# Starting the expert scatter one up-projection slab earlier, in a kernel for two transformer blocks

## The reference, cut to what matters

```
u   = expert_u[experts]                       # (256, 128, 1024)
act = gelu(einsum('td,tkd->tk', x, u)) * gates
out = einsum('tk,tkd->td', act, expert_v[experts])
```

## Time and profile before

| | us |
|---|---|
| median of three runs | 1771.59 |
| lowest, highest | 1768.38, 1773.86 |
| profiled execution, its time | 1774.22 |
| profiled execution, its span | 1772.6 |
| TensorE busy in the span | 1700.1 (96%) |
| VectorE, ScalarE busy | 1304.3 (74%), 1023.6 (58%) |
| first and last scatter matmul start | 525.3, 764.5 |
| mean granted TensorE clock | 0.987 |

### The profile page before, as it was taken

The page is one execution under the profiler, slowest core; times in us unless marked ns, Lnnn a source line. Parts: engine busy times, 40 slices in busy tenths (PEclk is TensorE's granted clock), DMA queues, the critical chain, the costliest instruction groups (busy, mean ns, idle before and its releaser), DMA issues.

```text
span 1772.6 us, 34483 instructions
## 1 busy us (share of the span) xinstructions
PE 1700.1 (96%) x10902; PEld 1530.1 (86%) x10902; DVE 1304.3 (74%) x2376; ACT 1023.6 (58%) x1567; POOL 119.5 (7%) x105
## 2 busy tenths in 40 slices
PE   7999999999999999999999999998999998899997
PEld 6998889999999999988888888897878887778886
DVE  5865755599977777767777777777777676877776
ACT  6753445566656666655445545663476666666665
POOL 0012300143320000000000000000000000000000
PEclk9998999999999999999999999999999999999999
DMA  5442246476775555567787777542345655246553
GB/s 189 163 158 72 82 138 212 150 230 199 218 236 176 177 175 172 172 206 241 244 270 243 239 244 242 172 150 84 107 155 192 196 181 158 84 131 201 190 186 111
DMA packets 114411, 316.65 MB, mean 179 GB/s; under 512 B 12752, under 2 KB 45904, under 8 KB 113840
## 3 DMA queue, kind: packets, MB, share of 16 engines
q1 hardware_dynamic: 113504, 311.88, 54.5%
q0 software_dynamic: 848, 4.00, 0.7%
HBM read 296.95 MB, written 18.87 MB: 178 GB/s over the span
## 4 chain that ended last, share of the span: by engine, by line
PE 82%; DVE 10%; ACT 4%; issue 2%; DMA 1%; POOL 1%; ACTq 0%; DVEq 0%; SPq 0%
PE bank L309 10%; PE bank L310 10%; PE bank L311 10%; PE bank L259 9%; PE bank L260 9%; PE bank L281 9%; PE bank L261 9%; PE bank L285 5%; PE bank L1302 3%; DVE wlo L243 2%; PE bank L1744 1%; ACT whi L235 1%; PE bank L1009 1%; POOL wlo L1601 1%; DVE arena L2023 1%
## 5 line engine op out<-in xcount | busy, mean ns | idle before, releaser
L243 DVE TENSOR_TENSOR wlo<-raw,whi 128x1024 fp32r<-128x1024 f32 x495 | 608.3, 1230 | 160.5 <-ACT whi L235 150.3
L235 ACT ACTIVATE whi<-raw 128x1024 fp32r<-128x1024 f32 x524 | 550.1, 1051 | 33.0 <-PE bank L303 20.5
L259 PE MATMUL bank<-x,whi 128*128 128x256 f32 (+1 forms) x1728 | 510.3, 295 | 8.9 <-DVE wlo L243 4.0
L261 PE MATMUL bank<-x,wlo 128*128 128x256 f32 (+1 forms) x1728 | 493.8, 286 | 0.0
L260 PE MATMUL bank<-x,whi 128*128 128x256 f32 (+1 forms) x1728 | 493.5, 286 | 0.0
L259 PEld LDWEIGHTS bank<-x,whi 128*128 128x128 f32 x1728 | 333.8, 193 | 15.2 <-issue 13.1
L260 PEld LDWEIGHTS bank<-x,whi 128*128 128x128 f32 x1728 | 334.2, 193 | 0.1
L261 PEld LDWEIGHTS bank<-x,wlo 128*128 128x128 f32 x1728 | 333.3, 193 | 0.0
L309 PE MATMUL bank<-whi,yhi 128*128 128x512 f32 x816 | 321.7, 394 | 8.7 <-DVE ylo L2215 3.0
L310 PE MATMUL bank<-wlo,yhi 128*128 128x512 f32 x816 | 320.3, 393 | 0.0
L311 PE MATMUL bank<-whi,ylo 128*128 128x512 f32 x816 | 319.9, 392 | 0.0
(11 more groups left out here) (306 smaller groups left out, 1755.7 us busy)
## 6 DMA issues: line engine op xcount, KB each, us to landing
raw<-in_stream SPq DMA_DIRECT2D x524, 512.0 KB, 3.5
act_spill<-h SPq DMA_DIRECT2D x128, 128.0 KB, 3.2
h<-act_spill SPq DMA_DIRECT2D x128, 128.0 KB, 3.2
h<-in_x SPq DMA_DIRECT2D x1, 1024.0 KB, 5.3
arena<-in_keys POOLq DMA_DIRECT2D x1, 1024.0 KB, 5.8
h_spill<-h SPq DMA_DIRECT2D x1, 1024.0 KB, 7.8
arena<-h_spill POOLq DMA_DIRECT2D x1, 1024.0 KB, 7.5
arena<-in_g_final POOLq DMA_DIRECT2D x1, 512.0 KB, 9.3
```

Source lines behind the costliest of these rows:

```text
L235: nc.scalar.activation(whi[:, q * 1024:(q + 1) * 1024], raw[:, q * 1024:(q + 1) * 1024], ACT.Copy).then_inc(hi_ready, 1)
L243: nc.vector.tensor_tensor(wlo[:, q * 1024:(q + 1) * 1024], raw[:, q * 1024:(q + 1) * 1024], whi[:, q * 1024:(q + 1) * 1024].bitcast(F32), ...
L259: nc.tensor.matmul(bank[b][:, 0:T], whi[:, w], xhi[:, x], start=k == 0, stop=False)
L261: last = nc.tensor.matmul(bank[b][:, 0:T], wlo[:, w], xhi[:, x], start=False, stop=k == KT - 1)
```

## The change

The 64 scatter steps ride on slabs 63 to 126 instead of 64 to 127, and all that prepares them (gates, transposes, columns) comes one slab earlier. Slab 127 is a plain `up` between the last step and `down`(0). ScalarE's queue gets `split_hi` of slab 130 ahead of the last `g_out`, and the gelu of slab 127 behind the first `y_step`. VectorE's last scatter step splits slab 129; the split of slab 130 moves from the last scatter step to a place behind `prod_lo`(0), ahead of `prod`(1).

```diff
-        E1 = 64
+        TPS = 4
+        SCAT = SEQ // TPS
+        E1 = KEYS - 1 - SCAT
         COLS_AT = E1 - 4
-        TPS = SEQ // (KEYS - E1)
...
             pe.sem_inc(s("hot_free"), TPS)
-            steps(pe, KEYS - E1, 4, step)
+            steps(pe, SCAT, 4, step)
+            up(pe, N_U + KEYS - 1, U_U + KEYS - 1, 0, 0, 4, SEQ)
             down_pe(pe, N_V, D_V, KEYS)
...
-            steps(act, KEYS - E1 - 1, 4, step2)
-            g_out(0, KEYS - E1 - 1)
+            steps(act, SCAT - 1, 4, step2)
+            split_hi(act, N_U + KEYS - 1 + AHEAD, 0, 0, 4)
+            g_out(0, SCAT - 1)
...
             y_step(N_V, D_V, 0, 0)
+            gelu(N_U + KEYS - 1, U_U + KEYS - 1, 0, 0)
...
-            steps(dve, KEYS - E1 - 1, 4, step)
-            last = KEYS - E1 - 1
+            steps(dve, SCAT - 1, 4, step)
+            last = SCAT - 1
             for y in range(TPS):
                 one_token(last // 4, last % 4, y)
                 if y == 1:
-                    split_lo(dve, N_U + KEYS - 1 + AHEAD, 0, 0, 4)
+                    split_lo(dve, N_U + KEYS - 2 + AHEAD, 0, 0, 4)
...
-            dve.wait_ge(s("g_evac"), KEYS - E1 + 2)
+            dve.wait_ge(s("g_evac"), SCAT + 2)
             prod(0, 0, 0)
             prod_lo(0, 0, 0)
+            split_lo(dve, N_U + KEYS - 1 + AHEAD, 0, 0, 4)
             prod(1, 0, 0)
```

## The result

Over 20 runs of each kernel the changed one takes 1776.12 us (median, 1772.45 to 1777.91) and the one before 1772.82 us; the ratio is 1.0018 with a 95% interval of 1.0011 to 1.0026. That is 3.2 us slower (0.0018 x 1772.8; the interval is 2.0 to 4.6), small but clear of noise at 20 runs, and under the 0.3% that three could tell. The forecast was +2.7, and 1774.3 us; of the 1.8 us between that and 1776.12, 1.2 is the kernel before, whose median is 1772.82 over 20 runs and was 1771.59 over three.

A forecast was written before the change was run, and what follows sets the result against it. TensorE, 82% of the chain that ended last, was taken to bound the kernel. Pauses of 1.6 and 3.8 us and one slow `down` (1.69) replace a 4.31 us hand-over: +2.7, 1774.3 us, range 1769.8 to 1777.0.

The forecast's parts named there:

- The head: Start of the scatter, one slab sooner: gates ready with 2.4 us of cover, so no cost.
- The first wait: Ahead of `down`(0): `prod`(0) waits for read-back 0, a pause of about 1.6 us; `down`(0) starts 1.1 us sooner.
- The second wait: Ahead of `down`(1): slab 130's late split holds SP's load and read-back 1; pause 3.8 us, `down`(1) 1.05 us later.
- The clock: TensorE in `down`(1): the 3.8 us pause drops the clock, the 1.6 us one does not; 1.69 us, between 0 and 1.69.
- Sum +2.7: At the start of `down`(2): 777.29 after against 774.55 before, +2.7 us.
- Rival 1: Second pause costs less, by a landing after 2.1 us or a clock staying up; about 1772.6 us, chance 0.25.
- Rival 4: Scatter's head: gates come late, after 508.9, and TensorE waits; +1 to +3 us on top, chance 0.04.
- Rival 3: Lateness passed on to `down`(4) through the load of slab 135 and read-back 4; 1778 us, chance 0.08.
- Rival 2: Read-back 1 lands by 767.5, `down`(0) and (1) at full clock; 1768.8 us, or 1767.3 without first wait, chance 0.08.

The follow-up runs named there:

- e5: The changed kernel with read-back 0 alone issued ahead of the store of 126; hand-over 19.12 us in one run (changed kernel 19.24).
- e6: The changed kernel with the last `g_out` ahead of the rounding of slab 130 on ScalarE; hand-over 19.62 us in one run (changed kernel 19.24).
- e1: The changed kernel with VectorE's split of slab 130 put back ahead of the first product; ratio 0.9991 to the kernel before.
- e7: The changed kernel with 15 extra, unused matmuls on TensorE between `down`(0) and `down`(1); ratio 1.0007 to the kernel before.
- e4: e8 plus the last `g_out` ahead of slab 130's rounding, that rounding behind the first `y_step`, VectorE's split of 130 behind `prod`(1); ratio 0.9986 to before.
- e8: The changed kernel with read-backs 0 to 2 issued early and the store of 127 ahead of the load of slab 134; ratio 0.9979 to before.
- e2: The changed kernel with read-backs 0 to 2 issued early, ahead of the load of slab 134 and the store of 127; ratio 0.9989 to before.
- e3: The kernel before with read-backs 0 to 2 issued early and nothing else; ratio 1.0012 to the kernel before.
- e9: The kernel before with read-backs 0 to 2 issued early, the same as e3, measured again; ratio 0.9990 to the kernel before.

## Why the prediction was right

- **The head costs nothing.** Right. TensorE is busy for 14.50 of 14.50 us there.
- **The first wait is read-back 0, 1.6 us.** Right: 1.66, and e5 and e6 show the read-back and not `g_out` as its cause.
- **The second wait is the split of slab 130 behind `prod_lo`(0), through SP's queue.** Right, with 3.95 us for 3.8. The split starts at 766.02 (766.11 forecast), the load at 767.27 (767.36), the read-back at 768.12 (768.14). These come so close in part because this execution ran 0.18 us ahead of the forecast at the last pair; counted from there they are 0.09, 0.09 and 0.16 late. e1 takes this one step back and the loss is gone. The landing was mis-sized: 3.66 us and not 3.2. The prediction took the median of the later read-backs because a slab stands ahead of them too; how far ahead it stands was left out, and e1 suggests that it counts. The prediction's figure of 2.0 us from the Trainium skill ("DMA: Bandwidth & Descriptors", section "Anatomy of one DMA") stands there for transfers that GpSimd issues, and these are issued by SP; no term hangs on it.
- **The clock falls after the second pause and not after the first, 1.69 us.** Right as to the place: 4.13 + 3.06 - 2 x 2.72 = 1.75 us, over two `down`s and not one; e7 gives 1.65. The size was luck in part: it was bounded at 1.69, and e5 and e6 paid 2.94 and 2.59 behind shorter pauses. The two limits behind it, 1.92 and 2.03 us, are those of one trace and don't hold in all the others (last section).
- **Sum +2.7.** Measured +3.27 in the trace, 0.53 more than the 2.74 of the sum. From the last pair (forecast at 764.18 - 2.88 = 761.30) to `down`(1) it was to be 11.58 us and is 12.05. The 0.47 are: read-back 0 landed in 2.61 us and not 2.5, 0.11; from the load of slab 134 to read-back 1 it was 0.85 and not 0.78, 0.07; read-back 1 landed in 3.66 and not 3.2, 0.46; from `prod`(1) to `down`(1) it was 1.39 and not 1.54, -0.15; the other steps give -0.02. The clock adds 1.75 - 1.69 = 0.06. Told by the pauses, the same 3.27 is 1.66 + 3.95 - 2.62 = 2.99, the clock's 0.06, -0.03 at the start of the first pause, and 0.25 in `down`(0), which takes 2.97 us and not 2.72 (0.09 at its first matmul, as in e4 and e8, and 0.16 for the end of its last one, which no other follows). The forecast left the 0.25 out, but that is not why the sum fell short: `down`(1) waits for read-back 1 whatever `down`(0) takes.
- Rival 1 (a cheaper second pause) did not happen: the landing was longer than forecast and the clock fell. Rival 4 (a late head) did not either. Rival 3 (lateness passed on to `down`(4)) did not happen: from `down`(3) on, 2.72 us each. Rival 2 did not happen in this kernel, and e8 shows what it would have needed: the read-backs ahead of slab 134.

## What to carry to other kernels

When work is moved behind a wait on one engine, follow what its completion releases: here an idle-looking VectorE split held SP's load, and a store and three read-backs stood behind that load in SP's list. A queue that runs in order wants its entries in the order of need, and by these traces a transfer that is needed soon does not belong close behind a large one. Cover for a wait at a hand-over pays only if the next wait down the chain is early too; look for the second one before counting the first. And a price of the clock that was read from one pause of one trace is a sample: give it a range.

## What the hardware showed that I had not expected

The price of the clock after almost the same pause differs. After 3.95 us of standing still the low stretch began 1.4 us into `down`(1) and cost 1.75 us. After 3.68 us in e5 and 3.80 us in e6, `down`(1) ran at 0.50 from its first matmul to its last. The windows of `down`(1) and (2) in e5:

```profile
771.59:776.88 5.29, 5.29 (x13) 4.18 (x14) 3.33 (x5) 1.69 (x3) 0.00 (x0) 0.50 0.48 173
776.88:779.97 3.09, 3.09 (x14) 2.52 (x12) 1.99 (x3) 1.37 (x2) 0.00 (x0) 0.89 0.44 171
```

That is 5.29 + 3.09 - 5.44 = 2.94 us, and in e6 5.27 + 2.76 - 5.44 = 2.59. It is why e5 comes out only 0.12 us better than the changed kernel. I had bounded this term at 1.69. In the other direction, every pause up to 1.77 us in these hand-overs (e1, e2, e5 to e8 and the changed kernel) left the clock at 1.00.

Outside the hand-over that does not hold, and neither do the limits that the prediction read from the trace of before. e3 and e9 are the same kernel, run twice. Behind almost the same pause near 1230 us, the one execution kept the clock and the other lost it:

```profile
1232.64 3.84 PE L1749 MATMUL bank<-arena 128*128 128x128 f32 x32 [3.46 <-DVE arena L2012]
1232.64:1239.64 7.00, 7.00 (x47) 6.40 (x48) 3.83 (x4) 3.39 (x4) 0.00 (x0) 1.00 0.01 2
...
1231.64 5.28 PE L1749 MATMUL bank<-arena 128*128 128x128 f32 x32 [3.49 <-DVE arena L2012]
1231.64:1238.64 7.00, 7.00 (x41) 6.67 (x42) 3.81 (x4) 3.12 (x3) 0.00 (x0) 0.78 0.01 2
```

The first two rows are of e3 and the last two of e9: the same 32 matmuls take 3.84 us and 5.28 us. And in e9 a pause of 1.73 us was followed by the low clock, where the same pause in e3 was not:

```profile
1294.58 1.06 PE L550 MATMUL bank<-ident,arena 128*128 128x128 f32 x8 [1.73 <-DVE arena L482]
1294.58:1300.58 6.00, 6.00 (x26) 4.30 (x27) 4.52 (x11) 5.58 (x12) 0.00 (x0) 0.72 0.00 0
```

In e1 and e7 the pause of 2.03 us near 1480 us, the shortest that had been followed by 0.50 before, left the clock at 1.00. So the length of a pause does not settle by itself what the clock does behind it. The Trainium skill ("TensorE: Matmul & The Clock Gate", section "What's actually happening") has it that the number of slow matmuls of one kernel varies from run to run, there at a kernel's start; e3 and e9 agree, with 3.84 and 5.28 us for the same 32 matmuls behind a pause.
